# Delta net: gates and the first head's queries and keys projected from x times the norm's weight, the token's factor applied behind them

## What is computed

```python
y = xf * lax.rsqrt(jnp.mean(xf * xf, axis=-1, keepdims=True) + RMS_EPS)
return (y * w.astype(jnp.float32)).astype(x.dtype)
...
proj = h @ w_in
qkv = jax.nn.silu(causal_depthwise_conv(proj[..., :3 * DN_WIDTH], conv_w))
z = proj[..., 3 * DN_WIDTH:4 * DN_WIDTH]
b = proj[..., 4 * DN_WIDTH:4 * DN_WIDTH + DN_HEADS]
a = proj[..., 4 * DN_WIDTH + DN_HEADS:]
...
beta = jax.nn.sigmoid(b.astype(jnp.float32))
g = -jnp.exp(a_log.astype(jnp.float32)) * jax.nn.softplus(a.astype(jnp.float32) + dt_bias.astype(jnp.float32))
```

## Time and profile before

| | us |
|---|---|
| median of 3 runs | 3491.51 (3486.74 to 3492.62) |
| the profiled execution | 3484.38 |
| its span in the trace | 3482.4 |
| PE busy | 3223.8 (93% of the span) |
| DVE / ACT / POOL busy | 1510.4 / 989.5 / 473.4 |

### The profile page before, as it was taken

How to read it: one execution, slowest core, us unless ns; L and a number is a source line. 1 busy time by engine, 2 the same in 40 slices (tenths; PEclk the granted TensorE clock), 3 DMA queues, 4 the chain that set the end, 5 groups by cost and what they waited for, 6 DMA issues and landing times. The chain is left out here.

```text
span 3482.4 us, 37739 instructions
## 1 busy us (share of the span) xinstructions
PE 3223.8 (93%) x15995; PEld 2635.9 (76%) x15995; DVE 1510.4 (43%) x1725; ACT 989.5 (28%) x1281; POOL 473.4 (14%) x335
## 2 busy tenths in 40 slices
PE   7899999998989999999967999989879899999998
PEld 5778877777868888888755665778768788888886
...
DMA packets 77240, 185.09 MB, mean 53 GB/s; under 512 B 7056, under 2 KB 28944, under 8 KB 77072
## 3 DMA queue, kind: packets, MB, share of 16 engines
...
## 5 line engine op out<-in xcount | busy, mean ns | idle before, releaser
L486 PE MATMUL ps<-b 128*128 128x512 f32 x5928 | 1468.8, 399 | 33.5 <-DVE b L1137 14.9
L486 PEld LDWEIGHTS ps<-b 128*128 128x128 f32 x5928 | 1095.6, 190 | 249.0 <-issue 17.8
L1333 PE MATMUL ps<-b 128*128 128x512 f32 x2592 | 608.5, 395 | 0.5 <-DVE b L1464 0.5
L1333 PEld LDWEIGHTS ps<-b 128*128 128x128 f32 x2592 | 485.0, 187 | 119.1 <-DVE b L1464 1.0
L475 DVE TENSOR_TENSOR b<-b 128x1024 fp32r<-128x1024 f32 (+1 forms) x206 | 271.7, 1321 | 372.8 <-ACT b L467 366.2
L2627 PE MATMUL ps<-b 128*128 128x512 f32 (+1 forms) x1584 | 363.0, 385 | 37.2 <-DVE b L1687 14.4
L467 ACT ACTIVATE b<-b 128x1024 fp32r<-128x1024 f32 (+1 forms) x206 | 215.1, 1046 | 564.6 <-PE ps L1333 464.2
L2627 PEld LDWEIGHTS ps<-b 128*128 128x128 f32 x1584 | 282.8, 196 | 94.8 <-issue 42.7
L1202 POOL TENSOR_TENSOR b<-b 128x1024 f32<-128x1024 f32 x24 | 57.4, 2393 | 1646.2 <-ACT b L1208 1645.8
L1048 POOL TENSOR_TENSOR b<-b 128x512 f32<-128x512 f32 x112 | 150.8, 1361 | 516.1 <-DVE b L952 398.2
L1379 ACT ACTIVATE b<-ps 128x1024 f32<-128x1024 f32 x54 | 55.4, 1025 | 389.2 <-PE ps L486 389.2
...
## 6 DMA issues: line engine op xcount, KB each, us to landing
b<-in_down SPq DMA_DIRECT2D x52, 512.0 KB, 3.7
...
b<-in_gu SPq DMA_DIRECT2D x44, 512.0 KB, 3.6
b<-scratch SPq DMA_DIRECT2D x38, 512.0 KB, 4.4
b<-in_dn_in SPq DMA_DIRECT2D x32, 512.0 KB, 5.0
b<-in_up SPq DMA_DIRECT2D x32, 512.0 KB, 3.8
b<-in_win SPq DMA_DIRECT2D x26, 512.0 KB, 4.0
scratch<-b SPq DMA_DIRECT2D x18, 512.0 KB, 3.0
```

The costliest lines, as they stand in the source:

```text
L486: ins = e.matmul(ps[:, c], w, h[:, k, c], start=first and k == 0 and i == 0, stop=last and k == KT - 1 and i == 2)
L1333: ins = e.matmul(ps[:, c], w, u[:, at[k], c], start=k == 0 and p == 0, stop=k == n - 1 and p == 2)
```

## The change

SP issues the parameters first, then x and the first weights by turns, and the constants and masks behind. ACT multiplies a tile of x by the norm's weight while it makes the high part, DVE makes the low part, and PE runs unit 0 (q) and the gates (now 32 columns, high and low weights side by side, four matmuls a tile) over these, and unit 1 (k) one tile behind. ACT's squares are summed on POOL, and PE sums only the sum and the last square over the features. When the factor is spread, the tiles are normed for units 2 and 3 (v and z) by `tile`: DVE multiplies, ACT takes the high part into the place where the un-normed tile was, and DVE (tile 0) or POOL (tiles 1 to 7) the low part. q and k get the factor behind (`scale`, on the evicted rows), the gates on 128x8x16. `first` sets the order of head 0's side work: v and z together, tile by tile.

```diff
+    def first(self):
+
+        on = self.on
+        on.tile(0)
+        on.tile(1)
+        on.done(0, 0, 0)
+        on.scale(0)
+        on.unit(2)
+        for k in range(KT + 1):
+            if k + 2 < KT:
+                on.tile(k + 2)
+            if k < KT:
+                for part in range(2):
+                    on.piece(2, k, part)
+                    yield None
+            if k == 0:
+                on.done(1, 0, 1)
+                on.scale(1)
+                on.unit(3)
+            else:
+                for part in range(2):
+                    on.piece(3, k - 1, part)
+                    yield None
+            if k < 2:
+                self.taps += [(0, k, t) for t in range(5)]
+            if k == KT - 1:
+                on.done(2, 0, 2)
+                self.taps += [(0, 2, t) for t in range(5)]
+        on.done(3, 0, 3)
+        self.ready.add((0, 3))
+
     def projections(self):
-        for h in range(H1):
+        yield from self.first()
+        for h in range(1, H1):
...
-            self.d_whi, self.d_wlo = (sb([128, 128], F32R, ph) for _ in range(2))
+            self.d_wc = sb([128, KT, 32], F32R, ph)
             self.d_masks = sb([128, 7 * 128], ctx=ph)
+            self.d_acc, self.d_sq = self.d_set[1][0], self.d_set[1][1:3]
+            self.d_gt = self.d_z[1][:, 0:256].rearrange("p (b c) -> p b c", c=32)
...
+    def sp_start(self, e):
+        x = lambda k: e.dma_start(self.d_x[:, k, :], self.a["x"][:, k, :]).then_inc(*self.xl[k].up("n1"))
+        e.dma_start(self.params, self.a["par"]).then_inc(*self.parl.up())
+        x(0)
+        self.sp_weights(e, 1)
+        x(1)
+        self.sp_weights(e, 2)
+        x(2)
+        e.dma_start(self.con_t, self.a["con"]).then_inc(*self.const.up())
+        for k in range(3, KT):
+            x(k)
+        self.sp_weights(e, 3)
+        e.dma_start(self.d_masks, self.a["masks"][0]).then_inc(*self.maskl.up("delta"))
...
+    def pe_start(self, e):
+        P, A, V, G = self.n1
+        S = self.psl[3]
+        for k in range(KT + 1):
+            if k == KT - 1:
+                e.wait_ge(*self.const.at())
+                e.wait_ge(*G.at("acc", KT - 2))
+                col_sums(e, self.psl[2], self.d_acc, self.con("ones"), True, False)
+                e.wait_ge(*A.at("sq", KT - 1))
+                col_sums(e, self.psl[2], self.d_sq[1], self.con("ones"), False, True).then_inc(*P.up("cs"))
+            if k < KT:
+                e.wait_ge(*V.at("l0", k))
+                if k == 0:
+                    e.wait_ge(*self.ww.at(0))
+                for part in range(2):
+                    ins = self.gemm_piece(e, self.psl[0], 0, k, part, self.b_hi, self.b_lo)
...
+                for i, h in enumerate((self.b_hi, self.b_lo)):
+                    for half in range(2):
+                        c = slice(512 * half, 512 * half + 512)
+                        ins = e.matmul(S[0:32, c], self.d_wc[:, k, :], h[:, k, c], start=k == 0 and i == 0,
+                                       stop=k == KT - 1 and i == 1)
+                if k == KT - 1:
+                    ins.then_inc(*P.up("gt"))
+            if k == KT:
+                e.wait_ge(*V.at("rc"))
+                rows(e, self.psl[2], self.st[:, 0:8], self.con("ident")).then_inc(*P.up("rw"))
+            if k:
...
+                for part in range(2):
+                    ins = self.gemm_piece(e, self.psl[1], 1, k - 1, part, self.b_hi, self.b_lo)
+                if k < KT:
+                    ins.then_inc(*P.up("k", k - 1))
+                else:
+                    ins.then_inc(*self.gm.up(1))
+
+    def act_start(self, e):
+        P, A, V, G = self.n1
...
+        def high(k):
+            e.wait_ge(*self.xl[k].at("n1"))
+            e.activation(self.b_hi[:, k, :], self.d_x[:, k, :], ACT.Copy,
+                         scale=self.par("norm_mix")[:, k:k + 1]).then_inc(*A.up("h0", k))
+
+        def square(k):
+            if k >= 2:
+                e.wait_ge(*G.at("acc", max(1, k - 2)))
+            e.activation(self.d_sq[k % 2], self.d_x[:, k, :], ACT.Square).then_inc(*A.up("sq", k))
+
+        e.wait_ge(*self.parl.at())
+        e.activation(self.d_wc[:, :, 0:16], self.par("wba").rearrange("p (k c) -> p k c", c=16), ACT.Copy).then_inc(*A.up("wba"))
+        for k in range(2):
+            high(k)
+            self.act_weights(e, k + 1)
+        for k in range(2):
+            square(k)
+        for k in range(2, KT):
+            high(k)
+            square(k)
+        self.act_weights(e, 3)
...
+    def dve_start(self, e):
+        P, A, V, G = self.n1
+        for b in self.d_pad:
+            e.memset(b[:, 0:3], 0.0).then_inc(*V.up("pad", b is self.d_pad[1]))
...
+        for k in range(KT):
+            e.wait_ge(*A.at("h0", k))
+            e.scalar_tensor_tensor(out=self.b_lo[:, k, :], in0=self.d_x[:, k, :], scalar=self.par("norm_mix")[:, k:k + 1],
+                                   in1=self.b_hi[:, k, :].bitcast(F32), op0=ALU.mult,
+                                   op1=ALU.subtract).then_inc(*V.up("l0", k))
+            if k < 2:
+                self.dve_weights(e, k + 1)
+        self.dve_weights(e, 3)
+        e.wait_ge(*P.at("cs"))
+        e.tensor_scalar(self.st[:, 0:8], self.psl[2][:, 0:1024:128], 1.0 / D, EPS, ALU.mult, ALU.add).then_inc(*V.up("ms"))
+        e.wait_ge(*A.at("rt"))
+        e.reciprocal(self.st[:, 0:8], self.st[:, 8:16]).then_inc(*V.up("rc"))
+        e.wait_ge(*P.at("rw"))
+
+    def pool_start(self, e):
+        P, A, V, G = self.n1
+        for k in range(1, KT - 1):
+            e.wait_ge(*A.at("sq", k))
+            if k > 1:
+                e.wait_ge(*G.at("acc", k - 1))
+            e.tensor_tensor(self.d_acc, self.d_sq[0] if k == 1 else self.d_acc, self.d_sq[k % 2],
+                            ALU.add).then_inc(*G.up("acc", k))
+        for k in range(1, KT):
+            e.wait_ge(*A.at("h", k))
+            e.tensor_tensor(self.b_lo[:, k, :], self.d_sq[k % 2], self.b_hi[:, k, :].bitcast(F32),
+                            ALU.subtract).then_inc(*G.up("l", k))
...
+        R = S[:, 768:1024]
-        for k in range(KT):
-            e.wait_ge(*n1[3 if k % 2 else 2].at("l", k))
...
-            if k == KT - 1:
-                ins.then_inc(*P.up("gt"))
-            side.fill(2)
         side.fill(4)
         e.wait_ge(*A.at("bt"))
...
         ins.then_inc(*P.up("gtr"))
-        side.fill(6)
+        side.fill(8)
...
         e.wait_ge(*V.at("g4"))
         e.matmul(S[:, 512:576], self.con("triu"), flat(self.g1), start=True, stop=True).then_inc(*P.up("gc"))
-        side.fill(2)
+        side.fill(4)
...
+        e.wait_ge(*self.n1[0].at("gt"))
+        e.activation(bt[0:32, :], S[0:32, :], ACT.Copy).then_inc(*A.up("bt"))
         side.fill(4)
-        o = R[:, 0:128].rearrange("p (b c) -> p b c", c=16)
         e.wait_ge(*P.at("gtr"))
-        e.activation(self.beta, o[:, :, 0:8], ACT.Sigmoid).then_inc(*A.up("beta"))
+        e.activation(gt.rearrange("p b c -> p (b c)"), S[:, 768:1024], ACT.Copy).then_inc(*A.up("gt"))
+        e.wait_ge(*V.at("g1"))
+        e.activation(self.beta, gt[:, :, 0:8], ACT.Sigmoid).then_inc(*A.up("beta"))
         e.wait_ge(*V.at("g2"))
...
-        self.act_decay(e, 0)
         for h in range(H1):
             side.head = h
             side.until(h, 1 if h else 2)
+            if h == 0:
+                self.act_decay(e, 0)
...
+        e.wait_ge(*A.at("gt"))
+        e.tensor_tensor(gt[:, :, 0:16], gt[:, :, 0:16], gt[:, :, 16:32], ALU.add).then_inc(*V.up())
+        e.wait_ge(*V.last())
+        e.tensor_tensor(gt[:, :, 0:16], gt[:, :, 0:16], self.st[:, 0:8][:, :, None].broadcast_to([128, 8, 16]),
+                        ALU.mult).then_inc(*V.up("g1"))
+        e.wait_ge(*V.last())
+        e.tensor_tensor(t1, gt[:, :, 8:16], dtb, ALU.add).then_inc(*V.up())
...
     def piece(self, j, k, part):
+        if j == 2 and part == 0:
+            self.e.wait_ge(*self.k.n1[3 if k else 2].at("l", k))
...
     def unit(self, j):
-        self.k.act_weights(self.e, j + 3)
+        self.k.act_weights(self.e, j + 3 if j >= 4 else j + 2)
+
+    def tile(self, k):
+        s, e = self.k, self.e
+        P, A, V, G = s.n1
+        e.wait_ge(*(P.at("k", k) if k < KT - 1 else s.gm.at(1)))
+        e.wait_ge(*V.at("z", k))
+        e.activation(s.b_hi[:, k, :], s.d_sq[k % 2], ACT.Copy).then_inc(*A.up("h", k))
...
-            e.wait_ge(*A.at("ev", 4 * h + which))
+            e.wait_ge(*(V.at("scale", which) if c < 2 else A.at("ev", 4 * h + which)))
...
+
+    def tile(self, k):
+        s, e = self.k, self.e
+        P, A, V, G = s.n1
+        z = s.d_sq[k % 2]
+        if k >= 2:
+            e.wait_ge(*(G if k > 2 else V).at("l", k - 2))
+        e.scalar_tensor_tensor(out=z, in0=s.d_x[:, k, :], scalar=s.par("norm_mix")[:, k:k + 1], in1=s.psl[2],
+                               op0=ALU.mult, op1=ALU.mult).then_inc(*V.up("z", k))
+        if k == 0:
+            e.wait_ge(*A.at("h", k))
```

(49 more changed lines are left out.)

92 lines of the change are left out of this document (32 added, 60 removed).

## The result

| | before | after |
|---|---|---|
| median, same chips | 3489.36 (3483.45 to 3492.62, 12 runs) | 3499.55 (3494.71 to 3506.70, 12 runs) |
| ratio, 95% interval | | 1.0032 [1.0022, 1.0042] |
| profiled execution, its span | 3484.38, 3482.4 | 3495.97, 3494.2 |

A forecast was written before the change was run, and what follows sets the result against it. PE, busy for 93% of the span, was taken to bound the kernel, with idle time in the opening and almost none in head 0. +10.8 - 3.9 + 1.6 = +8.5 us on 3491.5 gave 3500.0, range 3489 to 3508.

The forecast's parts named there:

- the mark: Start of PE's matmul L666 (L737 after the change), used for comparison: predicted at 112.6 in place of 101.84, 10.8 us later.
- what comes back: Head 0 from recurrence step 3 on: 42 side matmuls already done give 3.9 us back (bounds 0 and 9.7).
- head 1 starting near 208: Sign to check in the changed profile: head 1's first matmul near 208, where it started at 201.2.
- The start, up to R: Opening until the norm's factor is spread in PSUM: first matmul at 10.3 us, spread done at 45.0.
- Tiles for v and z: From the factor's spread to L666's start: tiles normed one after the other, a chain of 67.6 us.
- From there on the two orders are alike up to step 3 of head 0's recurrence: From L666's start to head 0's third recurrence step: same order before and after, so no cost was entered.
- DVE against POOL: DVE passes meeting POOL's low parts: 0.4 us charged a meeting, within the sum's roundings.
- The clock at head 1's start: Idle time at head 0's end lowers the clock for head 1's first matmuls: 1.6 us lost.
- (1) all side work comes back: Head 0: the 42 matmuls give all 9.7 us back, net +1.1, 3492.6 us; chance 0.30.
- (2) tiles at POOL's pace: Tiles for v and z not held up by the gates' chain: 16 us faster, 3475.5 us; chance 0.08.
- (3) clock and lock: Between tiles, idle stretches lower PE's clock and POOL slows DVE: 6 us more, +14.5, 3506 us; chance 0.15.

The follow-up runs named there:

- e1: The changed kernel with three of DVE's side items moved ahead of its wait in the gates' chain: 3495.55 us, ratio 1.0028 to the kernel before.
- e4: The changed kernel with ACT making head 0's decay exp before v's silu instead of behind it: 3500.50 us, ratio 1.0030 to the kernel before.
- e0_after: The changed kernel itself, measured again beside the others: 3499.48 us, ratio 1.0040 to the kernel before.
- e2: The changed kernel with POOL making head 1's decay only after the last tap group of head 1's k: 3497.05 us, ratio 1.0034 to the kernel before.
- e6: The changed kernel with three head 0 edits: DVE's side items earlier, POOL's decay later, ACT's exp before v's silu: 3491.31 us, ratio 1.0006 to the kernel before.

## Why the prediction was right, and where it was wrong

The time (3500.0 against 3499.55) and the sign were right, but that the two agree to 0.5 us is luck. The kernel before stood 2.1 us lower than the median that I added to. In the profile the change costs 11.8, where the sum had 8.5: the mark +11.0 (+10.8), the stretch behind it +8.2 (nothing), what comes back -4.3 (-3.9), head 1 -1.6 (+1.6), the rest -1.5 (nothing). One term is missing and one has the wrong sign, and they partly hid each other. My sign for it, head 1 starting near 208, failed: it started at 216.06.

- *The start, up to R*: right. First matmul at 9.28 (10.3 predicted), six cold matmuls 2.90, 3.7 a tile, spread done at 44.07 (45.0). POOL and DVE kept PE's pace, as bounded, and did so by turns: from tile 4 on DVE's low part takes 3.42 and POOL's sum 3.20, one pair every 3.35 us, so DVE has 0.3 us a tile to spare.
- *Tiles for v and z*: right. Mark 112.82 against 112.6; the start was 0.9 shorter than in the sum and this stretch 1.2 longer. PE waited 5.70 for q's eviction and 6.42 for POOL's low part, tile 4's product started at 74.06 ("near 75"). e1 and e4 confirm two of its links by taking them out: 4.3 for the gates' sums, 3.3 for the exp's place behind v's taps (3.0 in the sum: silu of v, table load and exp).
- *"From there on the two orders are alike up to step 3 of head 0's recurrence"*: this is the step that failed. Each engine's order is alike but for the side work, and the side work is ahead by 42 matmuls; so other taps stand beside other POOL passes. It cost 8.2 us in the first profile and 6.8 in e0_after's, of which e2 gives 5.9 back by putting off POOL's decay alone; the 2.2 that are left then were not taken out by any run.
- *DVE against POOL, "0.4 a meeting"*: the price was too low where DVE is on PE's path. Measured here: 1.0 for L510 beside a mask, 3.6 for two taps beside the decay. The Trainium skill (SBUF — State Buffer, "SBUF: two separate sides") calls it an exclusive lock in which whichever starts first gets the ports "for the whole instruction; the other fully blocks". The trace agrees: each of the two taps, 1.3 alone, ended 1.1 us behind the POOL pass that it had to let pass, 6.21 us in all. I had cited that rule and used it for the opening alone, where DVE has time to spare.
- *What comes back*: -4.3 against -3.9. Right in sum, with steps of 1.9 to 2.2 from step 3 on, and in part by luck: steps 3 to 7 gave 2.9 (3.2), the head's end 0.3 (0.7), and steps 1 to 3 another 1.1 that the sum had not, where a wait of 0.95 in the kernel before was gone.
- *The clock at head 1's start*: +1.6 predicted. The rows show 1.2 (L728 1.06 and L732 1.82 in place of 0.60 and 1.06), and head 1 was 1.6 shorter all the same, because its later slow stretches were shorter (behind the waits of 2.1 and 1.1 us six L521 took 1.78, six L486 2.91 before). Over these runs head 1 of the changed kernel, in one order, took 101.35 to 105.51.
- *The 1.5 us that the rest gave back* have no cause that I can name: they lie within the 2664.7 to 2666.3 us that the part behind head 7 takes in most profiles.
- *Rivals*: (1) all side work comes back: no, 4.3 of 9.7. (2) tiles at POOL's pace: no; even with both chain links out the mark is at 106.36 (e6). (3) clock and lock: its total (+14.5) was nearest to head 1's +14.9, though its place was wrong. Ahead of the mark both happened, as the turns above and a granted clock of 0.85 and 0.77 in the windows show, but the mark came where the sum had it. They cost time in head 0.

So the change swaps idle time of PE at the front (7.6 us more busy time there) for a longer chain through DVE, ACT and POOL. The chain bounds the mark, since x is now normed tile by tile behind the evictions and the gates' table loads.
